# The last two weight chunks of w_down, done token tile by token tile

## What is computed

```python
def conv_ffn(z, hist, w_up, cw, cb, w_down):
    ext = jnp.concatenate([hist, z @ w_up], 1)
    h = causal_dwconv(ext, cw, cb)
    g, v = jnp.split(h, 2, axis=-1)
    return (jax.nn.gelu(g, approximate=True) * v) @ w_down, ext[:, -(FFN_CONV_WIDTH - 1):]
...
    f, ffn_state = conv_ffn(rmsnorm(x, g_ffn_pre), ffn_hist, w_up, ffn_conv_w, ffn_conv_b, w_down)
    x = x + rmsnorm(f, g_ffn_post)
```

## Time and profile before

| | us |
|---|---|
| median of 3 runs | 997.74 |
| the runs | 1001.23, 995.15, 997.74 |
| the profiled execution, its own time | 992.95 |
| its span | 991.3 |
| TensorE busy | 943.6 (95%) |
| VectorE busy | 578.3 (58%) |
| ScalarE busy | 394.7 (40%) |

### The profile page before, as it was taken

The page is one execution under the profiler, slowest core; times in us unless marked ns, Lnnn a source line. Parts: engine busy times, 40 slices in busy tenths (PEclk is TensorE's granted clock), DMA queues, the critical chain, the costliest instruction groups (busy, mean ns, idle before and its releaser), DMA issues.

```text
span 991.3 us, 17745 instructions
## 1 busy us (share of the span) xinstructions
PE 943.6 (95%) x6757; PEld 856.8 (86%) x6757; DVE 578.3 (58%) x1077; ACT 394.7 (40%) x719; POOL 209.3 (21%) x275
## 2 busy tenths in 40 slices
PE   4999999996999999899999999999999999999995
PEld 2899999996888878799787999999999997777774
DVE  4448688998565654477456566666666664113114
ACT  5212163544454534442243444555555543212112
POOL 6443243454233323132000011111111110000000
PEclk9999999998999999999999999999999999999998
DMA  7665542331100000152511222222222222232212
GB/s 217 142 188 181 132 94 79 96 86 43 51 23 2 23 23 22 44 181 86 154 52 44 64 85 85 80 73 80 85 85 85 85 85 85 65 100 67 82 64 95
DMA packets 110897, 84.58 MB, mean 85 GB/s; under 512 B 12978, under 2 KB 97850, under 8 KB 110776
## 3 DMA queue, kind: packets, MB, share of 16 engines
q1 hardware_dynamic: 104368, 65.64, 23.0%
q0 software_dynamic: 4048, 15.19, 5.4%
q10 hardware_dynamic: 2426, 2.98, 1.0%
HBM read 78.71 MB, written 7.18 MB: 87 GB/s over the span
## 4 chain that ended last, share of the span: by engine, by line
PE 88%; DVE 4%; ACT 3%; DMA 2%; issue 2%; POOL 1%; POOLq 0%; ACTq 0%; DVEq 0%; SPq 0%
PE ps L1569 24%; PE ps L1570 24%; PE ps L1571 24%; PE ps L1856 2%; PE ps L1833 2%; PE ps L1639 2%; PE ps L1793 1%; DVE yc L1214 1%; DMA page<-in_state_kv_win_dram 1%; PE ps L1604 1%; PE ps L1796 1%; DMA raw<-in_w_out_dram 1%; DVE wl L1145 1%; PE ps L1690 1%; PE ps L1799 1%
## 5 line engine op out<-in xcount | busy, mean ns | idle before, releaser
L1569 PE MATMUL ps<-z,wh 128*128 128x288 f32 x704 | 209.4, 297 | 3.3 <-DVE z L1474 3.3
L1570 PE MATMUL ps<-z,wh 128*128 128x288 f32 x704 | 208.4, 296 | 0.0
L1571 PE MATMUL ps<-z,wl 128*128 128x288 f32 x704 | 207.6, 295 | 0.0
L1145 DVE TENSOR_TENSOR wl<-raw,wh 128x1024 fp32r<-128x1024 f32 (+1 forms) x67 | 87.9, 1313 | 167.2 <-ACT wh L771 167.1
L771 ACT CAST wh<-raw 128x1024 fp32r<-128x1024 f32 (+1 forms) x67 | 69.6, 1040 | 274.2 <-PE ps L1571 260.9
L1569 PE MATMUL ps<-zh,wh 128*128 128x288 f32 (+1 forms) x560 | 174.8, 312 | 0.8 <-ACT g L926 0.7
L1570 PE MATMUL ps<-zl,wh 128*128 128x288 f32 (+1 forms) x560 | 166.2, 297 | 0.0
L1571 PE MATMUL ps<-zh,wl 128*128 128x288 f32 (+1 forms) x560 | 166.0, 296 | 0.0
L1569 PEld LDWEIGHTS ps<-z,wh 128*128 128x128 f32 x704 | 132.5, 188 | 3.7 <-issue 2.1
L1571 PEld LDWEIGHTS ps<-z,wl 128*128 128x128 f32 x704 | 133.2, 189 | 0.0
L1570 PEld LDWEIGHTS ps<-z,wh 128*128 128x128 f32 x704 | 132.8, 189 | 0.0
(11 more groups left out here) (278 smaller groups left out, 1575.5 us busy)
## 6 DMA issues: line engine op xcount, KB each, us to landing
raw<-in_w_up_dram SPq DMA_DIRECT2D x44, 512.0 KB, 3.8
raw<-in_w_in_dram SPq DMA_DIRECT2D x30, 512.0 KB, 3.9
raw<-in_w_down_dram SPq DMA_DIRECT2D x22, 512.0 KB, 3.5
page<-in_cache_kv_dram POOLq DMA_DIRECT2D x16, 256.0 KB, 3.0
raw<-in_w_out_dram SPq DMA_DIRECT2D x8, 512.0 KB, 3.6
x<-in_x_prompt_dram SPq DMA_DIRECT2D x4, 512.0 KB, 5.3
page<-in_state_kv_win_dram POOLq DMA_DIRECT2D x16, 128.0 KB, 2.9
raw<-in_w_in_dram SPq DMA_DIRECT2D x8, 256.0 KB, 3.5
```

The source lines that it names most:

```text
L1145: nc.vector.tensor_tensor(wl[:, s % 2, 0:n], raw[:, s % 2, 0:n], wh[:, s % 2, 0:n].bitcast(F32), ALU.subtract).then_inc(lo_done, 1)
L1569: nc.tensor.matmul(out, ah, bh, start=start, stop=False)
L1570: nc.tensor.matmul(out, ah, bl, start=False, stop=False)
L1571: return nc.tensor.matmul(out, al, bh, start=False, stop=stop)
```

## The change

`token_major` runs its loop over all 11 chunks in the first half, and over only 9 in the second. The last two (kc 9 and 10) are done like this: tile 0 and tile 1 with chunk 9; a wait for chunk 10's low part; tile 0 with chunk 10, tile 1 with chunk 10; then for each of the tiles 2, 3 and 4 chunk 9 and chunk 10 one after the other. All five tiles now count `tile_done` after their last matmul, and these two chunks no longer count `slot_used`. ScalarE's `square` waits in the second half for `d_tile` for all five tiles. (`square` with the other end, S_UP, isn't called in this kernel.)

```diff
@@ def square(i, half, s_end, junk_i, done):
-                if half == 1 and i < TT - 1:
-                    act.wait_ge(o_tile if s_end == S_UP else d_tile, i + 1)
+                if half == 1:
+                    act.wait_ge(d_tile, i + 1)
                 else:
                     act.wait_ge(slot_used, s_end)
@@ def token_major(s0, kn, lhs, lhs_ok, bank4, taken, tile_done, after):
+                def tile_mm(half, kc, i):
+
+                    s = s0 + half * (kn // 2) + kc
+                    for kk in range(2):
+                        k = 2 * kc + kk
+                        mm = three(ps[0:ROWS[i], (half * TT + i) % 8, :],
+                                   (lhs[0][:, k, i * P:i * P + ROWS[i]], lhs[1][:, k, i * P:i * P + ROWS[i]]),
+                                   (whc[:, s % 2, kk, :], wlc[:, s % 2, kk, :]), k == 0, k == kn - 1)
+                    return mm
+
                 for half in range(2):
-                    for kc in range(kn // 2):
+                    for kc in range(kn // 2 - 2 * half):
                         s = s0 + half * (kn // 2) + kc
                         pe.wait_ge(lo_done, s + 1)
                         pe.wait_ge(lhs_ok, 2 * kc + 2 + AHEAD)
@@
-                            for kk in range(2):
-                                k = 2 * kc + kk
-                                mm = three(ps[0:ROWS[i], bk % 8, :],
-                                           (lhs[0][:, k, i * P:i * P + ROWS[i]], lhs[1][:, k, i * P:i * P + ROWS[i]]),
-                                           (whc[:, s % 2, kk, :], wlc[:, s % 2, kk, :]), k == 0, k == kn - 1)
-                            if half == 1 and kc == kn // 2 - 1 and i < TT - 1:
-                                mm.then_inc(tile_done, 1)
+                            mm = tile_mm(half, kc, i)
                         mm.then_inc(slot_used, 1)
                         after(half, kc)
+                pe.wait_ge(lo_done, s0 + kn - 1)
+                pe.wait_ge(lhs_ok, kn + AHEAD)
+                tile_mm(1, kn // 2 - 2, 0)
+                tile_mm(1, kn // 2 - 2, 1)
+                pe.wait_ge(lo_done, s0 + kn)
+                for i in range(TT):
+                    if i >= 2:
+                        tile_mm(1, kn // 2 - 2, i)
+                    tile_mm(1, kn // 2 - 1, i).then_inc(tile_done, 1)
```

## The result

| | before | after |
|---|---|---|
| median of 20 runs each | 996.38 us | 993.38 us |
| the runs lie between | 991.18 and 1003.66 | 989.90 and 995.08 |
| ratio, 95% interval | | 0.9963 [0.9948, 0.9979] |
| span of the profiled execution | 991.3 | 988.5 |

By the ratio the changed kernel is faster by 0.37%, with an interval from 0.21% to 0.52%, that is 2.1 to 5.2 us of 996.38. The quotient of the two medians alone is 0.9970, or 0.30%, and lies within that interval. 995.0 was forecast and 993.38 measured. The median of the kernel before moved too, from 997.74 in the three runs to 996.38 in twenty, so the two differences are the ones to compare: 2.75 forecast, 3.0 measured.

What follows compares the result with a forecast made beforehand. TensorE, busy 95% of the span, was taken as the bound, with only the end behind its last matmul movable. VectorE's end gains 2.75 us, the wait costs nothing: 997.74 - 2.75 = 995.0 us, range 991.8 to 998.8.

Steps and rivals of the forecast that it cites:

- What the change can move: End of the kernel: only what stands behind the last matmul can move; TensorE does nothing for the last 10.20 us.
- The matmuls' new times: Last two w_down chunks, second half: tiles 0 and 1 complete 4.09 us earlier, tile 2 2.73, tile 3 1.36, tile 4 unchanged.
- path (b): Behind the matmuls, through tile 3's square and product and tile 2's addition: VectorE's end at 984.50 us.
- The wait: TensorE's 13th matmul needs chunk 10's low part at 970.01, written by 969.85: cost nothing, bounds 0 and 0.3 us.
- The three paths: Three chains behind the matmuls, through tile 1 and the table load, tile 3, or tile 4; the latest sets VectorE's end.
- Path (c): Through tile 4's last matmul, square and product: VectorE's end at 985.19 us, latest by 0.69.
- path (a): Through tile 1, the table load and the first addition: VectorE's end at 983.85 us if VectorE were then never idle.
- The sum: VectorE's end gains 2.75 us, span 988.55, profiled execution 990.2; against the median of 997.74 this gives 995.0.
- R1: Kernel's end: queued writes of the five output tiles, not VectorE, end the kernel; nothing gained, 997.7 us; chance 0.07.
- R2: ScalarE or VectorE have something ahead of tile 0's square until 975.67, so tiles come no earlier: 997.7 us; chance 0.06.
- R3: Ahead of the 13th matmul: a wait of 4.10 us, then clock loss of 1.7 us, giving 1000.8 us; chance 0.04.
- The tail: From VectorE's end to the span's end, where the last outputs land: keeps its form, left at 3.36 us.

Runs made afterwards that it cites:

- early root: One more single-element root on ScalarE behind its last weight copy, moving the table load: VectorE's end 20.02 us on the kernel before, 17.98 on the changed kernel.
- split addition: Changed kernel with tile 3's addition cut in two halves and its root ahead of tile 4's square: VectorE's end 17.38 us, ratio 0.9966 to the kernel before.
- late weights: Changed kernel with four 128x1024 copies on ScalarE ahead of its copy of chunk 10: VectorE's end 23.83 us after chunk 9's start, whole execution 1000.44 us.

## Why the prediction was right

The time alone would not show it. The range of 991.8 to 998.8 us also holds the 997.7 of a change that does nothing, and the gain is smaller than the spread of the runs. 993.38 lies 1.6 us under the 995.0, and 1.36 of that is the median of the kernel before, which came down with more runs. What bears the prediction out is the replay of the end, step by step:

- *What the change can move.* Right: it is the stretch behind the last matmul. TensorE's share of the two chunks went from 13.41 to 13.45 us.
- *The matmuls' new times.* The last matmuls of the tiles were put at 971.15, 972.51, 975.23, 977.96 and 980.70. A square starts 0.43 later (0.39 for the matmul, 0.04 to the square; 0.44 for tile 4), and 0.17 is upstream, which gives 971.41, 972.77, 975.49, 978.22 and 980.97. The profile has the squares at 971.43, 972.80, 975.52, 978.24 and 981.01. In its last part the prediction adds the 0.4 to 981.1 as well, which already held it; that was a slip of the text and not of the sum. Another slip is in the forecast's own bounds: had path (b) been the end (984.50), VectorE would have gained 3.44 us, and the time would be 994.3 and not 994.7. The forecast and the measurement's place in the range don't hang on it.
- *The wait.* Taken at 0 with bounds of 0 and 0.3. The last matmul starts 13.45 to 13.49 us after chunk 9's start in the four kernels that have the close wait and nothing else on TensorE, against 13.41 with three tiles ahead, so it costs 0.04 to 0.08. The margin of 0.16 us that the rows before gave is there in the changed kernel too (write done 2.56 us after chunk 9's start, matmul due at 2.72), and what lies beyond it is dear: the kernel with one tile ahead, where the write comes too late, gave back 1.34 us of the gain. The changed kernel works on a narrow edge here. An order with three tiles ahead ends at the same time with 1.36 us more of this margin, but with nothing to spare on the path through the first addition.
- *The weight load behind a wait* (the Trainium skill, "TensorE: Matmul & The Clock Gate", section "Step-by-step: what each phase is for"). The page states that weight loads are pulled ahead of the matmuls in flight. That this ends at a wait is the prediction's own step, not the page's. The trace of the changed kernel agrees with both: elsewhere in the stream the load for a matmul starts together with the matmul ahead of it (the first and second of chunk 9: both 967.12), and the load behind the wait starts at 969.73, 0.05 after VectorE's write ends (968.45 + 1.23 = 969.68), where without the wait it would have started at 969.62. But its matmul starts at 969.84, on time, and the one after it 0.23 later, not 0.33 as was taken from the row of a matmul released after a real pause. The prediction's estimate of 0.11 us for a load of 128 columns, from the page's figure, differs from the trace, which records 0.19 us for each; the trace decides. Of the tenth of a microsecond that the wait might have cost, 0.04 is left at the last matmul.
- *The three paths.* Path (c) was forecast as the latest. It is: VectorE idles 0.60 us ahead of tile 4's product (about 0.6 was to be seen; the 0.69 of the replay is counted from when a busy VectorE would have started it, and is 981.72 - (979.84 + 1.20) = 0.68 in the profile), and an earlier first addition moves nothing (early root, 17.98). In the kernel before path (a) was the latest, and 0.63 of its load of 1.28 us counted.
- *The sum.* 2.75 forecast, 2.71 in the profile from chunk 9's start to VectorE's end. The whole span went down by 2.8, 0.17 of it not from the change. The medians differ by 3.0, within the interval of the ratio; what of this is more than 2.7 can't be told from spread.
- *R1* fell: with an output left out the tail is 3.49. *R2* fell: the first square started 4.24 us earlier, 0.17 of it upstream. *R3* didn't come about, because the write is in time; made to happen, it cost 4.16 + 1.72 us, with 4.2 + 1.7 expected of that kernel. What R3 had wrong is its break-even of 1.05 us, which charges the whole clock term to a short pause too: the kernel with one tile ahead paused for 1.25 us, kept its clock at 1.00 and still ended 1.37 us before the kernel before did.
- *The pace.* The prediction named one thing that it had taken without a row: that 12 matmuls in a row to the same bank run at the pace of 6. They do: tile 3's twelve take 2.72 us and 0.227 each.
- *What was less exact.* The tail was left at 3.36 and is 3.44. In the other kernels it lies between 3.37 and 3.49, with spans known to 0.1, so no effect of the order can be seen in it.

## What to carry to other kernels

Where a matmul engine that is never idle feeds several tiles to slower engines behind it, the order of the last matmuls decides how much work is left after the last one, at no cost in matmul time. Write down when each tile becomes complete in the old and new order, replay the consumers' queues from the rows, and take the latest path: finishing tiles early pays only until the path through the last tile is the longest, and from there on the next gain lies in what is queued ahead of that last tile's work. Look at which write the reordered wait now meets, and with what margin; where there is a choice of orders with the same end, weigh that margin against the slack on the other paths (here three tiles ahead gives the first and takes the second).

## What the runs showed that I had not expected

The start of chunk 9's first matmul lies between 965.76 and 972.57 us in ten profiled executions, whose programs do the same work up to that point. That is 6.8 us, more than twice what the change gives, while from there to VectorE's end each kernel for which an end was expected came within 0.1 us of it. In these executions the spread thus comes from ahead of the changed stretch; that it's the same in the runs without a profile is likely and not shown. It goes with TensorE's granted clock: these are rows of the view of core, span and mean granted clock of the kernel with an output left out, which starts chunk 9 first, and of the one with the split addition, which starts it last.

```profile
core 0: 987.2 us, clock 0.989
```

```profile
core 0: 993.4 us, clock 0.984
```

In between the order is roughly kept: the changed kernel has 0.988 and starts the chunk at 967.12, the kernel before with the early root 0.987 and 967.15, the kernel before 0.986 and 967.29, the one with four tiles 0.987 and 969.14, and the kernels with three tiles, one tile and the early root in the changed order all 0.984, with starts from 970.77 to 971.20. (The kernel with late weights, 0.985 and 971.60, has a low stretch behind the chunk's start as well.) An estimate from the two rows above is (0.989 - 0.984) x 990 = 5 us, 4 to 6 within the rounding of the clocks, of the 6.8. So the clock goes along with the start and can be most of it; that it is the whole cause isn't shown. The earlier trace rows show such a stretch at the low level, behind a stretch with TensorE busy for less than half. The traces also give a place: the split kernel's granted clock is 0.94 from 260 to 280 us and 0.91 from 520 to 540, where the kernel with an output left out has 1.00 in both. Which pauses bring such stretches in one execution and not in another was not tried.
